# Feed-forward stages of a two-block decoder kernel: the norm's factor per token multiplied in after the up projection

## Chip, cores and metric

The kernel runs on one core of one Trainium2 chip. The metric is the device time of one execution in microseconds (us). The kernel before takes 2204.48 us, the median of 3 runs from 2202.61 to 2205.71.

## What is computed

One sequence of 256 tokens with model width 1024 goes through a first block (feed-forward, state-space mixer, two feed-forwards, attention, feed-forward) and a second block (two mixers and a layer of experts). The change is in the four feed-forward stages, each of which computes

```python
def rmsnorm(x, g):
    xf = x.astype(jnp.float32)
    y = xf * lax.rsqrt(jnp.mean(xf * xf, axis=-1, keepdims=True) + EPS)
    return (y * g.astype(jnp.float32)).astype(x.dtype)

def swiglu_half_step(h, g, w1, w3, w2):
    u = rmsnorm(h, g)
    return h + FFN_HALF * ((jax.nn.silu(u @ w1) * (u @ w3)) @ w2)
```

with h of 256 x 1024, w1 and w3 of 1024 x 2816 and w2 of 2816 x 1024. The stages in order are ffn0, ssm, ffn1, ffn2, kv, attn, ffn3, rwkv, mla, mix, peer. The keys and values come from the h that goes into ffn2, normalised with a gain of their own: TensorE transposes ffn2's normalised rows a second time at ffn2's end (`kv_turn`).

## The kernel before

**Split products.** Every fp32 matrix is held as a rounded part (hi) and a rest (lo), and a product is three matmuls: hi·hi, hi·lo, lo·hi. A weight tile (128 x 1024) comes by DMA into one of four ring slots. ScalarE writes `w_hi[slot]` (`make_hi`, L298), VectorE subtracts to get `w_lo[slot]` (`make_lo`, L303), TensorE multiplies. Each slot has one w_hi and one w_lo: the next tile of the slot is split only when the last product that reads it is done (`split_read`). For a stage's second tile (slot 1) the subtraction at its start is done by GpSimd (`POOL_LEADS`), and for its first tile (slot 0) both halves are made at the end of the stage before. In ffn3 ScalarE makes the hi of slot 1 only after the norm's roots (`LEAD_AFTER_ROOTS`), since the attention stage frees that slot late.

**A feed-forward stage** has 22 tiles of 128 hidden columns. TensorE's order is up(t), down(t-1), up(t+1), down(t), ...: up is 48 matmuls of 256 columns (w1 in slot 0, then w3 in slot 1) into one PSUM bank, down is 12 matmuls of 512 columns (w2 in slot 2 or 3) into four accumulator banks. Between them ScalarE takes silu of the w1 half (L687) and VectorE multiplies it by the w3 half (L709, L710) and splits the result (L712); that is `gate`. At the stage's end the order is up(21), three quarters of down(20), three quarters of down(21), then both last quarters. VectorE adds each finished quarter to h (`update_h`, L592).

**The entry of a stage** (`norm_scalar`, `norm_vector`, `norm_tensor`, `project_first`). h is handled in four quarters: q0 and q1 are the two halves of the width for the first 128 tokens, q2 and q3 for the other 128. ScalarE squares and sums each quarter (L469), and takes Ln and Exp for the factor of each token (L475, L478). VectorE multiplies the rows by it (`rows`, L509, into norm_u), TensorE transposes them (L573), VectorE turns q0 and q2 into `u_hi` with the gain (L514), ScalarE q1 and q3 (L490), VectorE makes `u_lo` of all four in the order q0, q2, q1, q3 (L521, four instructions each). TensorE runs 8 matmuls on zeros ahead of the transposes and 4 between their halves (`keep_busy`, L555). `project_first` then takes tile 0: for w1 and then for w3 eight pairs (L333, L335) with u_hi, the fifth of which waits for ScalarE's quarters; then 16 matmuls with u_lo (L340), the fifth of which waits for all of u_lo. When the first 8 of these are done, slot 0 can be split again for tile 1, and with that the loop begins (L351).

The order on each engine is the order of the code; engines meet only in semaphores.

Of the kernel before, what the change touches and what calls it, by code (L numbers as in the profile page):

```python
# [199 lines left out]
def program(nc, io, stages=STAGES):  # L200
# [31 lines left out]
    with ctx:  # L232
# [230 lines left out]
        def norm_scalar(act, s):  # L463
            m, split = norm_no[s], s in SPLIT_STAGES
            for q in range(4):
                tt = q // 2
# [17 lines left out]
            act.wait_ge(S("in_loaded"), 32)  # L484
            to = u_t if s in PLAIN_STAGES else u_hi
            turned_at = TURNED_OF.get(s, TURNED)
            for q in (1, 3):
                act.wait_ge(S("norm_turned"), 4 * m + q + 1)
                for c in range(4):
                    ins = act.activation(quarter(to, q)[:, c, :], turned_at[q][:, c * P:(c + 1) * P], ACT.Identity,  # L490
                                         scale=V(GAIN[s], 4 + c, 5 + c))
                ins.then_inc(S("u_turned"), 1)
                if s == stages[0]:
                    lead_scalar(act, s, slice(0, 1) if q == 1 else slice(1, None))
# [2531 lines left out]
```

## Time and profile before

| | |
|---|---|
| runs, median of 3 | 2204.48 us (2202.61 to 2205.71) |
| profiled execution, its own time | 2207.05 us |
| its span | 2205.3 us |
| TensorE busy | 2160.1 us, 98% |
| VectorE busy | 1466.5 us, 67% |
| ScalarE busy | 1020.1 us, 46% |
| GpSimd busy | 59.2 us, 3% |
| mean granted TensorE clock | 0.996 of full speed |
| the chain that ended last | 92% TensorE, 4% VectorE, 1% ScalarE |

All times of a trace are microseconds from the span's start. ffn0 enters its loop at 23.6, ffn1 at 411.9, ffn2 at 605.9, ffn3 at 901.6. The page names instructions by the line of the kernel, the engine and what they write and read. "Idle before" in square brackets is how long the engine stood before an instruction, and who released it. The chain of waits lists only what held up the end. The granted clock is given as a share: 1.00 is 2.4 GHz and 0.50 is 1.2 GHz.

### The profile page before, as it was taken

How to read it: one execution, taken by the hardware profiler on the slowest of the kernel's cores; microseconds unless marked ns; L12 is line 12 of the kernel's file. 1: busy time of each engine (PE TensorE's matmuls, PEld its weight loads, DVE VectorE, ACT ScalarE, POOL GpSimd, SP SyncE). 2: the span in 40 equal slices, each digit the busy share in tenths (PEclk: the TensorE clock that was granted, in tenths of full speed). 3: DMA queues.
4: the chain of work that ended last, by engine and by line, in shares of the span. 5: the costliest groups of instructions: out<-in, count | busy, mean ns of one | idle time of the engine just before them, and what ended most of it. 6: DMA issues, size and time to landing. Idle time of an engine off the chain costs nothing.

```text
span 2205.3 us, 42309 instructions
## 1 busy us (share of the span) xinstructions
PE 2160.1 (98%) x15414; PEld 1941.0 (88%) x15428; DVE 1466.5 (67%) x2785; ACT 1020.1 (46%) x1734; POOL 59.2 (3%) x59
## 2 busy tenths in 40 slices
PE   8999999999999999999999899999999999999999
PEld 7999998899899987899998568889889999999998
DVE  5556997655655556655685577989886666666665
ACT  4435766443534346434552353348634444444443
POOL 0000000000010000000000000100000000000000
PEclk9999999999999999999999999999999999999999
DMA  6555664455476534555531024443567666665564
GB/s 210 182 189 176 210 189 143 159 177 192 148 239 199 193 116 141 163 188 182 189 97 52 20 77 146 141 145 138 206 229 234 218 204 207 202 189 189 183 189 134
DMA packets 107726, 374.14 MB, mean 170 GB/s; under 512 B 11984, under 2 KB 17888, under 8 KB 107376
## 3 DMA queue, kind: packets, MB, share of 16 engines
q1 hardware_dynamic: 102848, 354.88, 49.2%
q0 software_dynamic: 4784, 18.00, 2.8%
q8 instruction: 59, 0.97, 0.2%
q14 instruction: 35, 0.29, 0.0%
HBM read 362.29 MB, written 13.69 MB: 170 GB/s over the span
## 4 chain that ended last, share of the span: by engine, by line
PE 92%; DVE 4%; ACT 1%; DVEq 1%; issue 1%; DMA 1%; POOL 0%; ACTq 0%; SPq 0%
PE bank L351 71%; PE bank L380 8%; PE bank L1574 3%; PE bank L2583 3%; DVE w_lo L303 1%; PE bank L555 1%; PE bank L573 1%; ACT w_hi L298 0%; PE bank L2151 0%; PE bank L333 0%; DVE u_lo L521 0%; PE bank L335 0%; PE bank L2535 0%; PE bank L2158 0%; DVE arena L1965 0%
## 5 line engine op out<-in xcount | busy, mean ns | idle before, releaser
L303 DVE TENSOR_TENSOR w_lo<-ring,w_hi 128x1024 fp32r<-128x1024 f32 x576 | 696.4, 1223 | 406.6 <-ACT w_hi L298 404.2
L298 ACT ACTIVATE w_hi<-ring 128x1024 fp32r<-128x1024 f32 x581 | 605.6, 1056 | 617.8 <-PE bank L351 563.9
L351 PE MATMUL bank<-u_hi,w_hi 128*128 128x256 f32 x2568 | 729.0, 284 | 1.9 <-DVE w_lo L303 1.9
L351 PE MATMUL bank<-u_hi,w_lo 128*128 128x256 f32 x2568 | 726.6, 283 | 0.0
L351 PE MATMUL bank<-u_lo,w_hi 128*128 128x256 f32 x2568 | 726.6, 283 | 0.0
L351 PEld LDWEIGHTS bank<-u_hi,w_hi 128*128 128x128 f32 x2568 | 492.1, 192 | 13.0 <-DVE w_lo L303 4.0
L351 PEld LDWEIGHTS bank<-u_lo,w_hi 128*128 128x128 f32 x2568 | 492.2, 192 | 7.4 <-issue 0.5
L351 PEld LDWEIGHTS bank<-u_hi,w_lo 128*128 128x128 f32 x2568 | 492.1, 192 | 0.0
L351 PE MATMUL bank<-w_hi,x_hi 128*128 128x512 f32 x992 | 391.0, 394 | 2.1 <-DVE x_lo L2789 1.3
L351 PE MATMUL bank<-w_lo,x_hi 128*128 128x512 f32 x992 | 388.3, 391 | 0.0
L351 PE MATMUL bank<-w_hi,x_lo 128*128 128x512 f32 x992 | 386.1, 389 | 0.0
L351 PEld LDWEIGHTS bank<-w_hi,x_hi 128*128 128x128 f32 x992 | 187.1, 189 | 39.6 <-issue 2.4
L351 PEld LDWEIGHTS bank<-w_hi,x_lo 128*128 128x128 f32 x992 | 186.4, 188 | 40.4
L351 PEld LDWEIGHTS bank<-w_lo,x_hi 128*128 128x128 f32 x992 | 187.2, 189 | 31.5
L380 PE MATMUL bank<-u_t,ring 128*128 128x256 f32 x928 | 206.1, 380 | 2.2 <-issue 1.8
L380 PEld LDWEIGHTS bank<-u_t,ring 128*128 128x128 f32 x928 | 174.0, 190 | 26.6 <-issue 3.2
L2786 DVE TENSOR_TENSOR x_hi<-arena 128x256 fp32r<-128x256 f32 (+1 forms) x128 | 54.5, 426 | 124.3 <-ACT arena L2649 113.9
L2649 ACT ACTIVATE arena<-bank 128x256 f32<-128x256 f32 x96 | 36.9, 385 | 179.6 <-PE bank L351 179.6
L1574 PE MATMUL bank<-arena 64*64 64x64 f32 (+1 forms) x1888 | 68.2, 229 | 7.6 <-DVE arena L1965 2.1
L1574 PEld LDWEIGHTS bank<-arena 64*64 64x64 f32 x1888 | 63.8, 137 | 13.2 <-ACT arena L1803 2.8
L2583 PEld LDWEIGHTS bank<-arena 128*128 128x128 f32 x512 | 60.2, 192 | 5.4 <-issue 4.0
L2583 PE MATMUL bank<-arena 128*128 128x128 f32 x512 | 62.1, 278 | 2.8 <-issue 1.5
(312 smaller groups left out, 1774.2 us busy)
## 6 DMA issues: line engine op xcount, KB each, us to landing
ring<-in_w SPq DMA_DIRECT2D x264, 512.0 KB, 3.6
ring<-in_expert_u SPq DMA_DIRECT2D x128, 512.0 KB, 3.5
ring<-in_expert_v SPq DMA_DIRECT2D x128, 512.0 KB, 4.2
ring<-in_ssm_in SPq DMA_DIRECT2D x40, 512.0 KB, 4.5
gate_dram<-con SPq DMA_DIRECT2D x16, 576.0 KB, 2.9
arena<-gate_dram POOLq DMA_DIRECT2D x9, 1024.0 KB, 8.5
ring<-in_ssm_out SPq DMA_DIRECT2D x16, 512.0 KB, 4.1
ring<-in_w_o SPq DMA_DIRECT2D x16, 512.0 KB, 3.7
```

The costliest lines, as they stand in the source:

```text
L298: act.activation(w_hi[slot][:, :], ring[slot][:, :], ACT.Copy).then_inc(hi_made[slot], 1)
L303: dve.tensor_tensor(w_lo[slot][:, :], ring[slot][:, :], w_hi[slot][:, :].bitcast(F32), ALU.subtract).then_inc(freed[slot], 1)
L351: mm = pe.matmul(out, left[a], right[b], start=start and n == 0, stop=stop and n == 2, skip_group_check=True)
L380: mm = pe.matmul(out, ring[slot][:, c * width:(c + 1) * width], u_t[:, c, :], start=(c == 0), stop=(c == DC - 1))
L555: pe.matmul(bank[4][:, :], zeros[:, 0:P], zeros[:, :], start=True, stop=True)
L573: mm = pe.transpose(TURNED_OF.get(s, TURNED)[q][:, c * P:(c + 1) * P], norm_u[:, q // 2, at:at + P], C("ident"))
L1574: mm = pe.matmul(bank[b][a, at:at + width], left[a, :], right[a, :], start=(n == 0), stop=(n == len(products) - 1))
L2583: mm = pe.matmul(ROT[g][:, t * P:(t + 1) * P], one_b[:, g, t, :], one_a[:, g, t, :], start=True, stop=True)
L2649: act.activation(gelu_buf[:, n, :], ROT[n][:, 0:T], ACT.Gelu).then_inc(S("gelu_out"), 1)
L2786: dve.tensor_tensor(chunks(x_hi[:, n:n + 1, :]), chunks(src), gates, ALU.mult)
```

## The change

For the four feed-forward stages (`LATE_SCALE`):

- TensorE transposes h itself, as soon as a quarter of h is updated; `rows` and the zero matmuls of the entry are gone (12 ahead of ffn0's transposes stay, and 4 behind them). ffn2 still makes its rows, for kv, but behind its u_lo.
- The products are made with h times the gain, without the factor per token. ScalarE writes the factors as a diagonal matrix of 128 x 128 for each half of the tokens (`diag`), TensorE multiplies it by ones between the fourth and fifth pair of the w3 tile (`spread_roots`), so that every partition of bank 0 holds the 256 factors, and VectorE copies that to `root_t`, ahead of the last quarter of u_lo.
- ScalarE squares the last quarter and takes the second root only after its two quarters of u_hi.
- In `gate`, VectorE first multiplies the whole up tile (512 columns: w1 and w3 halves) by root_t into SBUF (`scaled_up`), then ScalarE takes silu from there, then VectorE goes on as before. In the kernel before, silu read PSUM as soon as the tile was done.

```diff
+LATE_SCALE = ("ffn0", "ffn1", "ffn2", "ffn3")
...
         def project_first(pe, stage, *products, one_bank=False, between=None):
...
+                    if between and (n, c) == (1, 4):
+                        between()
...
         def norm_scalar(act, s):
             for q in range(4):
                 tt = q // 2
+                if late and q == 3:
+                    turned(1)
+                    turned(3)
...
-                    act.activation(stat[:, 10 + tt:11 + tt], stat[:, 8 + tt:9 + tt], ACT.Exp,
-                                   scale=-0.5).then_inc(S("norm_root"), 1)
+                    ins = act.activation(stat[:, 10 + tt:11 + tt], stat[:, 8 + tt:9 + tt], ACT.Exp, scale=-0.5)
+                    if late:
+                        act.drain()
+                        act.wait_ge(S("in_loaded"), 32)
+                        ins = act.activation(diag[:, tt, :], C("ident"), ACT.Copy, scale=stat[:, 10 + tt:11 + tt])
+                    ins.then_inc(S("norm_root"), 1)
             if s in LEAD_AFTER_ROOTS:
                 lead_scalar(act, s, slice(LEAD_BEFORE[s], 2))
...
+            if not late:
+                turned(1)
+                turned(3)
...
         def norm_vector(dve, s):
-            rows(0)
+            if s not in LATE_SCALE:
+                rows(0)
...
                 for q in (0, 2, 1, 3):
+                    if q == 3 and s in LATE_SCALE:
+                        dve.wait_ge(S("norm_turned"), turned_before(s) + 5)
+                        dve.tensor_copy(root_t, bank[0][:, 0:T])
                     lo(q)
+                if s == HOLDS_KV:
+                    rows(0)
+                    rows(1)
...
         def norm_tensor(pe, s):
-            elif not calm:
+            elif not calm and s not in LATE_SCALE:
                 keep_busy(pe, 8)
             for q in range(4):
-                if q == 2 and not calm:
+                if q == 2 and not calm and s not in LATE_SCALE:
                     keep_busy(pe, 4)
...
-                pe.wait_ge(S("norm_rows"), 4 * norm_no[s] + (4 if s == "attn" else q + 1))
+                if s in LATE_SCALE:
+                    pe.wait_ge(S(("h_loaded", "h_moved")[q // 2]), 16)
+                    pe.wait_ge(S("h_updated"), max(4 * upd[s] - 2 + q, 1))
+                else:
+                    pe.wait_ge(S("norm_rows"), rows_before(s) + (4 if s == "attn" else q + 1))
...
         def ffn_tensor(pe, k, updates):
+            def spread_roots():
+                for tt in range(TT):
+                    pe.wait_ge(S("norm_root"), 2 * norm_no[stage] + tt + 1)
+                    mm = pe.matmul(bank[0][:, tt * P:(tt + 1) * P], C("ones"), diag[:, tt, :], start=True, stop=True)
+                mm.then_inc(S("norm_turned"), 1)
...
         def ffn_scalar(act, k):
             def silu(b, i):
-                split_done(act, *ffn_tile(1, k, i, b))
-                act.activation(silu_buf[:, b, :], UP[b][:, 0:T], ACT.Silu).then_inc(S("silu_ready"), 1)
+                act.wait_ge(S("up_scaled"), FC * ffn_no[stage_of(k)] + 2 * i + b + 1)
+                act.activation(silu_buf[:, b, :], scaled_up[:, b, 0:T], ACT.Silu).then_inc(S("silu_ready"), 1)
...
         def ffn_vector(dve, k):
             def gate(b, i):
+                split_done(dve, *ffn_tile(1, k, i, b))
+                dve.tensor_tensor(scaled_up[:, b, :].rearrange("p (n t) -> p n t", n=2),
+                                  UP[b][:, :].rearrange("p (n t) -> p n t", n=2),
+                                  root_t.unsqueeze(1).broadcast_to([P, 2, T]), ALU.mult).then_inc(S("up_scaled"), 1)
                 dve.wait_ge(S("silu_ready"), base + 2 * i + b + 1)
...
-                dve.tensor_tensor(x_hi[:, b, :], silu_buf[:, b, :], UP[b][:, T:2 * T], ALU.mult)
-                dve.tensor_tensor(hid_buf[:, b, :], silu_buf[:, b, :], UP[b][:, T:2 * T], ALU.mult)
+                dve.tensor_tensor(x_hi[:, b, :], silu_buf[:, b, :], scaled_up[:, b, T:2 * T], ALU.mult)
+                dve.tensor_tensor(hid_buf[:, b, :], silu_buf[:, b, :], scaled_up[:, b, T:2 * T], ALU.mult)
```

The rest of the diff renames two semaphores of the state-space stage into one and counts the semaphores anew.

**ScalarE at ffn3's entry.** L469/L500 are the squares, L478/L509 the Exp, L490/L487 the quarters of u_hi, L298/L299 the hi of a weight tile (first slot 1, then slot 2). Before:

```order
L469 ACTIVATE arena,stat<-h 128x512 [waits h_updated,h_moved]
L475 ACTIVATE stat<-stat 128x1
L478 ACTIVATE stat<-stat 128x1
L298 ACTIVATE w_hi<-ring 128x1024 [waits split_read1,slot_full1]
L490 ACTIVATE u_hi<-bank,vec 128x128 [waits norm_turned,in_loaded]
L490 ACTIVATE u_hi<-bank,vec 128x128 x3
L490 ACTIVATE u_hi<-bank,vec 128x128 [waits norm_turned]
L490 ACTIVATE u_hi<-bank,vec 128x128 x3
L298 ACTIVATE w_hi<-ring 128x1024 [waits split_read2,slot_full2]
```

And now, L513 being a diagonal:

```order
L487 ACTIVATE u_hi<-bank,vec 128x128 [waits norm_turned]
L487 ACTIVATE u_hi<-bank,vec 128x128 x3
L487 ACTIVATE u_hi<-bank,vec 128x128 [waits norm_turned]
L487 ACTIVATE u_hi<-bank,vec 128x128 x3
L500 ACTIVATE arena,stat<-h 128x512 [waits h_updated,h_moved]
L506 ACTIVATE stat<-stat 128x1
L509 ACTIVATE stat<-stat 128x1
L513 ACTIVATE arena<-con,stat 128x128 [waits in_loaded]
L299 ACTIVATE w_hi<-ring 128x1024 [waits split_read1,slot_full1]
L299 ACTIVATE w_hi<-ring 128x1024 [waits split_read2,slot_full2]
```

The hi of slot 1 stood ahead of the quarters of u_hi; it now stands behind them, behind the last square, the second root and its diagonal.

**VectorE at ffn2's entry**, from its quarters of u_hi (L514/L541) on; L521/L548 is u_lo, L581 the copy of the spread factors, L509/L536 the rows. Before:

```order
L514 TENSOR_TENSOR u_hi<-bank,vec 128x4x128 [waits norm_turned]
L521 SCALAR_TENSOR_TENSOR u_lo<-bank,vec,u_hi 128x128 x8
L521 SCALAR_TENSOR_TENSOR u_lo<-bank,vec,u_hi 128x128 [waits u_turned]
L521 SCALAR_TENSOR_TENSOR u_lo<-bank,vec,u_hi 128x128 x3
L521 SCALAR_TENSOR_TENSOR u_lo<-bank,vec,u_hi 128x128 [waits u_turned]
L521 SCALAR_TENSOR_TENSOR u_lo<-bank,vec,u_hi 128x128 x3
L303 TENSOR_TENSOR w_lo<-ring,w_hi 128x1024 [waits hi_made2]
```

And now:

```order
L541 TENSOR_TENSOR u_hi<-bank,vec 128x4x128 [waits norm_turned] x2
L548 SCALAR_TENSOR_TENSOR u_lo<-bank,vec,u_hi 128x128 x8
L548 SCALAR_TENSOR_TENSOR u_lo<-bank,vec,u_hi 128x128 [waits u_turned]
L548 SCALAR_TENSOR_TENSOR u_lo<-bank,vec,u_hi 128x128 x3
L581 COPY arena<-bank 128x256 [waits norm_turned]
L548 SCALAR_TENSOR_TENSOR u_lo<-bank,vec,u_hi 128x128 [waits u_turned]
L548 SCALAR_TENSOR_TENSOR u_lo<-bank,vec,u_hi 128x128 x3
L536 TENSOR_SCALAR arena<-h,stat 128x512 [waits norm_root]
L536 TENSOR_SCALAR arena<-h,stat 128x512
L536 TENSOR_SCALAR arena<-h,stat 128x512 [waits norm_root]
L536 TENSOR_SCALAR arena<-h,stat 128x512
L304 TENSOR_TENSOR w_lo<-ring,w_hi 128x1024 [waits hi_made2]
```

The copy stands between the third and fourth quarter of u_lo and waits for TensorE. The four rows moved from ahead of u_hi to behind u_lo, and only in ffn2; the other three feed-forward stages have none.

**VectorE at the last tile of ffn0**, up to the update of h. Before:

```order
L709 TENSOR_TENSOR x_hi<-arena,bank 128x256 [waits split_read3,silu_ready]
L710 TENSOR_TENSOR arena<-arena,bank 128x256
L712 TENSOR_TENSOR x_lo<-arena,x_hi 128x256
L592 SCALAR_TENSOR_TENSOR h<-bank,h 128x512 [waits acc_done] x3
```

And now:

```order
L757 TENSOR_TENSOR arena<-bank,arena 128x512 [waits split_read1]
L762 TENSOR_TENSOR x_hi<-arena 128x256 [waits split_read3,silu_ready]
L763 TENSOR_TENSOR arena<-arena 128x256
L765 TENSOR_TENSOR x_lo<-arena,x_hi 128x256
L632 SCALAR_TENSOR_TENSOR h<-bank,h 128x512 [waits acc_done] x3
```

The multiplication by the factors (L757) is new; ScalarE's silu stands between it and x_hi.

## Rows read from the trace of the kernel before

**Rows 1.** The page: busy time of each engine.

```profile
PE 2160.1 (98%) x15414; PEld 1941.0 (88%) x15428; DVE 1466.5 (67%) x2785; ACT 1020.1 (46%) x1734; POOL 59.2 (3%) x59
```

**Rows 2.** Timeline, end of ffn1: start, duration, engine, line, out<-in.

```profile
588.00 0.38 ACT L687 ACTIVATE arena<-bank 128x256 f32<-128x256 f32 x1 [1.76 <-PE bank L351]
...
589.25 0.43 DVE L712 TENSOR_TENSOR x_lo<-arena,x_hi 128x256 fp32r<-128x256 f32 x1
...
589.64 0.40 PE L351 MATMUL bank<-w_hi,x_lo 128*128 128x512 f32 x1
...
589.88 0.40 PE L351 MATMUL bank<-w_hi,x_hi 128*128 128x512 f32 x1
```

**Rows 3.** Groups by shape: count | busy us, mean ns | idle before.

```profile
L514 DVE TENSOR_TENSOR u_hi<-bank,vec 128x512 fp32r<-128x512 f32 x12 | 8.3, 692 | 8.2 <-PE bank L573 8.2
...
L429 ACT ACTIVATE x_hi<-arena 128x256 fp32r<-128x256 f32 x8 | 3.2, 414 | 6.2 <-PE bank L351 6.2
```

**Rows 4.** Timeline, ffn2's end: VectorE turning the kv quarters.

```profile
785.35 1.29 DVE L733 TENSOR_TENSOR u_t<-bank,vec 128x512 f32<-128x512 f32 x2 [0.55 <-PE bank L619]
```

**Rows 5.** Timeline, middle of ffn1's loop, VectorE and ScalarE.

```profile
489.43 0.42 DVE L709 TENSOR_TENSOR x_hi<-arena,bank 128x256 fp32r<-128x256 f32 x1
...
491.68 1.06 ACT L298 ACTIVATE w_hi<-ring 128x1024 fp32r<-128x1024 f32 x1 [3.34 <-PE bank L351]
```

**Rows 6.** Chain of waits at ffn1's entry: start, us, what.

```profile
399.62 1.67 PE bank L555 x7
401.30 0.87 PE bank L573 x8
...
404.44 0.36 PE bank L333
...
408.51 0.97 PE bank L340 x8
...
409.57 1.07 ACT w_hi L298
...
410.66 1.24 DVE w_lo L303
```

**Rows 7.** Timeline, ffn1's entry, VectorE and ScalarE.

```profile
400.20 0.87 DVE L509 TENSOR_SCALAR arena<-h,stat 128x512 f32<-128x512 f32 x2
...
400.87 0.61 ACT L469 ACTIVATE arena<-h 128x512 f32<-128x512 f32 x1
...
402.01 0.20 ACT L478 ACTIVATE stat<-stat 128x1 f32<-128x1 f32 x1
...
404.40 4.23 DVE L521 SCALAR_TENSOR_TENSOR u_lo<-bank,vec,u_hi 128x128 fp32r<-128x128 f32 x16
```

**Rows 8.** Chain of waits at ffn3's entry.

```profile
889.24 1.67 PE bank L555 x7
...
901.56 23.49 PE bank L351 x170
```

**Rows 9.** Timeline, ffn3's entry, ScalarE and GpSimd.

```profile
891.74 1.04 ACT L298 ACTIVATE w_hi<-ring 128x1024 fp32r<-128x1024 f32 x1
892.69 2.15 ACT L490 ACTIVATE u_hi<-bank,vec 128x128 fp32r<-128x128 f32 x8
...
892.87 2.38 POOL L303 TENSOR_TENSOR w_lo<-ring,w_hi 128x1024 fp32r<-128x1024 f32 x1 [212.38 <-ACT w_hi L298]
```

**Rows 10.** Timeline, ffn0's entry, TensorE.

```profile
8.33 1.94 PE L573 MATMUL bank<-con,arena 128*128 128x128 f32 x8 [2.45 <-DMA vec<-in_vecs]
```

**Rows 11.** Stretches: busy (x) of PE, PEld, DVE, ACT, POOL; PEclk, DMA share, GB/s.

```profile
9.00:10.00 1.00, 1.00 (x6) 1.00 (x6) 0.47 (x1) 0.25 (x2) 0.00 (x0) 0.50 1.03 422
...
12.00:13.00 1.00, 1.00 (x10) 0.86 (x9) 0.56 (x1) 0.58 (x2) 0.00 (x0) 1.00 0.89 127
...
859.00:860.00 1.00, 0.62 (x3) 0.63 (x4) 1.00 (x4) 0.17 (x1) 0.00 (x0) 0.50 0.47 123
...
864.00:865.00 1.00, 1.00 (x4) 0.67 (x2) 0.00 (x0) 1.00 (x5) 0.00 (x0) 0.50 0.10 25
```

More of the change, by code:

```diff
@@ L323, in lead_next_hi, with project_first @@
                 lead_scalar(act, stage, slice(0, LEAD_BEFORE.get(stage, 0)))
-        def project_first(pe, stage, *products, one_bank=False):
+        def project_first(pe, stage, *products, one_bank=False, between=None):
             for n, (out, slot, ring_stage, i, nth) in enumerate(products):
@@ L453, in program, with rows_before, turned_before @@
         HOLDS_KV = "ffn2"
+        diag, root_t = area(20000, 2, P), area(20256, T)
+        scaled_up = area(20512, 2, 2 * T)
+        rows_made = [s for s in norm_no if s not in LATE_SCALE or s == HOLDS_KV]
+        def rows_before(s):
+            return 4 * len([x for x in rows_made if norm_no[x] < norm_no[s]])
+        def turned_before(s):
+            return 4 * norm_no[s] + len([x for x in LATE_SCALE if norm_no[x] < norm_no[s]])
         def quarter(u, q):
@@ L464, in norm_scalar, with turned @@
             m, split = norm_no[s], s in SPLIT_STAGES
+            late = s in LATE_SCALE
+            to = u_t if s in PLAIN_STAGES else u_hi
+            turned_at = TURNED_OF.get(s, TURNED)
+            def turned(q):
+                act.wait_ge(S("norm_turned"), turned_before(s) + q + 1)
+                for c in range(4):
+                    ins = act.activation(quarter(to, q)[:, c, :], turned_at[q][:, c * P:(c + 1) * P], ACT.Identity,
+                                         scale=V(GAIN[s], 4 + c, 5 + c))
+                ins.then_inc(S("u_turned"), 1)
+                if s == stages[0]:
+                    lead_scalar(act, s, slice(0, 1) if q == 1 else slice(1, None))
             for q in range(4):
                 tt = q // 2
+                if late and q == 3:
+                    turned(1)
+                    turned(3)
                 act.wait_ge(S(("h_loaded", "h_moved")[tt]), 16)
@@ L483, in norm_scalar @@
                 kv_squares(act)
[L484 to L494, printed above, removed]
+            if not late:
+                turned(1)
+                turned(3)
             if split and s in PLAIN_STAGES:
@@ L543, in norm_vector @@
                 turned(0, u_hi)
-                rows(1)
+                if s not in LATE_SCALE:
+                    rows(1)
                 turned(2, u_hi)
@@ L614, in kv_turn @@
         def kv_turn(pe, q):
+            if q == 0:
+                pe.wait_ge(S("norm_rows"), rows_before(HOLDS_KV) + 4)
             if q >= 2:
@@ L656, in down @@
                 close_split(pe, b, 2 + b, stage, i, last, quarters)
+            def spread_roots():
[3 more added lines that the diff above has]
+                mm.then_inc(S("norm_turned"), 1)
             pe.wait_ge(S("hid_ready"), base + 1)
-            project_first(pe, stage, *((UP[0][:, n * T:(n + 1) * T], *ffn_tile(n, k, 0, 0)) for n in range(2)), one_bank=True)
+            project_first(pe, stage, *((UP[0][:, n * T:(n + 1) * T], *ffn_tile(n, k, 0, 0)) for n in range(2)), one_bank=True,
+                          between=spread_roots)
             clear_acc(pe, updates)
```

14 lines of the change are left out of this document (8 added, 6 removed).

## Prediction, made blind

> **What bounds the kernel now.** I read the page first: TensorE is busy for 2160.1 of 2205.3 us, VectorE for two thirds, ScalarE for half [rows 1]. Inside the loops of a feed-forward stage the chain of waits is unbroken TensorE work. So only the seams can give time, and only what TensorE waits for there counts. Then I read the timeline and the chain around the four entries and four ends of the feed-forward stages, and last the granted clock where TensorE had stood idle.
>
> An end: TensorE issues the last of nine matmuls of down(20) at 589.64 and the first of down(21) at 589.88, on its normal pitch, while VectorE's x_lo ends at 589.68 [rows 2]. The cover is 0.2 us. An entry, counted from t = 0 when TensorE starts its zero matmuls (399.62): transposes at 1.7, first products at 4.8, products with u_lo from 8.9, the first half of these done at 9.9; then hi and lo of slot 0 (1.07 and 1.24), and the loop begins at 12.3 [rows 6]. ffn3 is the same, 889.24 to 901.56 [rows 8].
>
> **The change part by part.** I work in one clock, that of the profiled execution.
>
> *In the loop.* VectorE gets one more instruction per tile. A product of 512 elements from PSUM takes it 0.69 us [rows 3]. Each tile lasts 8.5 us (48 products at 0.12 and 12 at 0.23), of which VectorE works some 5 (three subtractions of 1.23 and 1.25 for gate). In the loop its gate starts at 489.43 when both weight subtractions are done, not when silu is. Now: scale 489.4 to 490.1, silu from SBUF (0.41, the like row of rows 3) to 490.6, three steps of gate (1.25 as from silu's end to x_lo's end less a hop) to 491.9. VectorE's next work waits for the hi that ScalarE starts at 491.68 and ends at 492.7 [rows 5], so 0.8 us are spare, and the down product needs gate's result only at about 494.5, after up(t+1). The loop costs nothing. Uncovered, all of it would be 88 x 0.69 = 61 us.
>
> *The ends.* There the same insertion has 0.2 us of cover. From the end of the last up product the chain was silu, x_hi, hid, x_lo (588.00 to 589.68 [rows 2]); it becomes scale, silu, x_hi, hid, x_lo. Added: 0.69, one hop between engines of 0.04 (silu's end 588.38 to the next engine's start is of this size), and 0.06 because silu and x_hi read SBUF. That is 0.8, less 0.2 of cover: 0.6 us each for ffn0, ffn1 and ffn3. ffn2 has the kv transposes in between; there VectorE's work on the kv quarters comes 0.8 later, and TensorE's third kv transpose waits for the first of them. These take 1.29 for two [rows 4]; I take 0.4. Ends together: 3 x 0.6 + 0.4 = +2.2. Below zero is excluded, as nothing at the ends is removed; at most it is 4 x 0.8 = 3.2.
>
> *ffn1's entry.* TensorE transposes q0 to q2 from t = 0, four in 0.44 (8 in 0.87 [rows 6]), so 1.3; q3 behind the update of h, to 1.75. VectorE's second u_hi is done at 2.3 and the first product starts at 2.4, against 4.8. ScalarE: diagonal 0.35 (estimated from a 128 x 128 piece of 0.28, four in 1.14), third square to 1.6, u_hi's two quarters to 3.75, then last square to Exp's end 1.34 (400.87 to 402.21 [rows 7]) and a second diagonal: 5.45. The fifth pair therefore waits for ScalarE until 3.8; the w3 tile's fourth pair is done at 5.9 and the factors are there. VectorE: three quarters of u_lo at 1.05 each (4.23 for four [rows 7]) from 2.3 to 5.5, then it stands until the spread product (5.9 to 6.2) has landed, copies (0.35, estimated from the 0.42 of x_hi with its overlap), and makes the last quarter from 6.75 to 7.8. TensorE's fifth u_lo product goes at 7.85, the half is done at 8.5 against 9.9. From there on hi and lo follow as before. Gain 1.4, not the 2.4 of the earlier start: the copy and its wait stand in front of the last quarter.
>
> *ffn2's entry.* The same, but four rows (0.87 for two [rows 7], so 1.75) now stand behind u_lo: 7.8 to 9.6, slot 2's subtraction to 10.8, and slot 0's to 12.0, where ScalarE's hi would have allowed 9.7. The loop begins at 12.1 instead of 12.5. Gain 0.4.
>
> *ffn3's entry.* Here the order on ScalarE decides. The hi of slot 1 ran at 891.74, t = 2.5, and GpSimd's subtraction from 892.87 for 2.38 us to t = 6.0 [rows 9]; the w3 tile started at about 7.0 (4.8, 16 pairs' halves at 0.12, and 0.25 for the first), so it had 1.0 us of cover. Now that hi stands behind u_hi's quarters, the last square, the root and its diagonal: 5.45 to 6.5, and GpSimd 6.6 to 9.0. TensorE's w1 pairs are done at 4.95, and it stands idle for 4.0 us. Then four pairs to 10.0, spread 10.25, copy 10.75, last quarter of u_lo 11.85, half done 12.55 against 9.9. That is +2.7.
>
> *The clock in ffn3.* In ffn0 TensorE stood 2.45 us ahead of its first transposes [rows 10] and found 1.2 GHz; it was back at 2.4 by 12 [rows 11]. In attention, after a stretch with many holes, it ran at 1.2 from 859 to 865 [rows 11]. A hole of 4.0 us should do the same. The pairs then take 0.24 instead of 0.12. If it recovers 3.3 us after work resumes, as in ffn0, half of w3's pairs and part of the rest are slow, +1.4; if after 6.4, as in attention, +2.8. Between 0 (it holds) and 2.8 I take 2.1.
>
> *ffn0's entry* is bound by its weights: slot 1's lo comes at 15.8 instead of 16.2, but the factor's copy takes 0.4 back. 0, within -0.3 to +0.5.
>
> *The zero matmuls.* Without them the entries of ffn1 and ffn2 have holes of 0.6 and 0.3 us between bursts of work. I cost them at nothing, since the transposes keep TensorE going for the first 1.75 us; what it costs if not is the second rival.
>
> **Sum.** Ends +2.2, ffn0 0, ffn1 -1.4, ffn2 -0.4, ffn3 +2.7 and +2.1: +5.2 us. The profiled execution would go from 2207.05 to 2212.2. It was itself 2.6 above the median of the runs, so the median goes from 2204.48 to 2209.7.
>
> **Rivals.**
>
> *A. The clock holds in ffn3's hole.* For it: the two low stretches followed the kernel's start and a stretch of many small holes, not a hole in the middle of dense work. Against it: the one clean hole there is, 2.45 us, was followed by 1.2 GHz, and this one is longer. +3.1, so 2207.6.
>
> *B. The clock falls at ffn1's and ffn2's entries as well.* This needs transposes not to keep it up: then TensorE does next to nothing that counts from t = 0 to 2.4, as long as in ffn0's hole. For it: in ffn0 eight transposes and four zero matmuls ran at the low clock before it rose, so the rows can't tell which of them raised it. Against it: the hole is filled, and products follow at 2.4. Each entry would lose what I took for ffn3, 2.1: +9.4, so 2213.9. The Trainium skill (page "TensorE: Matmul & The Clock Gate", Part 4, PE-mode transpose) states that the full clock "doesn't engage" for transposes, as they don't count as busy in the same way. By that rule this rival is the likely one. No row here shows transposes alone for long enough, so the trace neither agrees nor disagrees.
>
> *C. The other side: the entries are bound by their start.* If TensorE, not VectorE's copy, set the pace, ffn1, ffn2 and ffn3 would each be 2.4 us shorter. The point that decides is whether the w3 tile's lo is there at t = 5 in ffn3 and the last quarter of u_lo before TensorE gets to it, in ffn1 and ffn2. For it: the first product does start 2.4 earlier. Against it: VectorE's 4.2 us of u_lo already ended only just ahead of its readers, and GpSimd's 2.38 us can't start before ScalarE. 2.2 - 7.2 = -5.0, so 2199.5.
>
> *D. The loop does not hide the scale.* Every row of the loop leaves 0.8 us, but if the extra hop to ScalarE delayed the next hi by half a us per tile, 88 tiles would add 44 to the forecast: 2253.7.
>
> **How the numbers follow.** My forecast 0.52, A 0.13, B 0.22, C 0.09, D 0.04. A change within 0.2%, 4.4 us, can't be told from none in this kernel. The forecast's own spread is 2.5 either way (ends 0 to 3.2, clock 0 to 2.8, estimated copies and diagonals), from 2207.2 to 2212.2; about 0.3 of its 0.52 lies above 2208.9. Slower: 0.32 + B 0.22 + D 0.04 = 0.58. Same: 0.20 + A 0.13 + 0.02 of C = 0.35. Faster: 0.07. The range takes in A and B and leaves out most of C and D: 2204.0 to 2215.5.
>
> **What would show it.** In ffn3, TensorE idle about 4 us ahead of the first pair of the w3 tile, released by GpSimd's w_lo, and the loop beginning 15 to 17.5 us after t = 0; the clock at half behind it. In ffn1 the loop beginning near 10.9, with VectorE standing before its copy; in ffn2 near 12.1, with the rows between u_lo and slot 2. At the ends of ffn0, ffn1 and ffn3, TensorE waiting some 0.6 us for x_lo ahead of down(21). In the loops, spacing of 8.5 us per tile as before. I am wrong if slot 1's lo is there earlier in ffn3, if the low clock shows in ffn1 or ffn2, or if the loops got longer.

## The result, and the profile after

| | before | changed |
|---|---|---|
| median (lowest to highest), 12 runs each | 2203.64 us (2200.12 to 2205.71) | 2208.20 us (2206.02 to 2210.82) |
| ratio, 95% interval | | 1.0021 [1.0013, 1.0029] |
| profiled execution (span) | 2207.05 us (2205.3) | 2207.07 us (2205.3) |

The changed kernel is slower by 4.6 us, 0.21%. The forecast was +5.2 us and a median of 2209.7 (2204.0 to 2215.5).

The page of the changed kernel: VectorE has 58 us more work [rows 1], the 88 new scales above all, and TensorE 5 us less, since 36 zero matmuls are gone.

```profile
PE 2155.0 (98%) x15404; PEld 1938.5 (88%) x15404; DVE 1524.7 (69%) x2865; ACT 1035.3 (47%) x1742; POOL 59.3 (3%) x59
```

**An end.** The timeline of the changed kernel at ffn1's end, which answers to [rows 2]. L757 is the scale, L736 silu, L762 and L765 x_hi and x_lo, L354 the product.

```profile
585.80 0.69 DVE L757 TENSOR_TENSOR arena<-bank,arena 128x512 f32<-128x512 f32 x1 [0.37 <-PE bank L354]
...
586.53 0.42 ACT L736 ACTIVATE arena<-arena 128x256 f32<-128x256 f32 x1 [2.48 <-DVE arena L757]
...
586.98 0.43 DVE L762 TENSOR_TENSOR x_hi<-arena 128x256 fp32r<-128x256 f32 x1 [0.48 <-ACT arena L736]
...
587.44 0.39 PE L354 MATMUL bank<-w_hi,x_lo 128*128 128x512 f32 x1
587.81 0.43 DVE L765 TENSOR_TENSOR x_lo<-arena,x_hi 128x256 fp32r<-128x256 f32 x1
...
588.29 0.50 PE L354 MATMUL bank<-w_hi,x_hi 128*128 128x512 f32 x1 [0.46 <-DVE x_lo L765]
```

TensorE now stands 0.46 us before the last down product, where it stood not at all. The cost is a little more than the number in brackets: from the product before it, at 587.44, to this one are 0.85 us, where they were 0.24 in the kernel before. From the loop's start to the stage's last product ffn1 takes 182.11 us instead of 181.35, ffn3 182.07 instead of 181.35: +0.7 each, as in ffn0. ffn2, with its kv transposes in between, takes 0.6 more.

**ffn1's entry.** The chain of waits of the changed kernel, which answers to [rows 6]. The transposes start at 398.21, so t is the time less 398.21.

```profile
400.76 1.56 ACT u_hi L487 x6
...
402.37 0.39 PE bank L336
...
404.54 0.46 PE bank L703 x4
...
405.02 0.42 DVE arena L581
405.44 1.04 DVE u_lo L548 x4
...
406.53 0.76 PE bank L343 x4
...
409.74 0.51 PE bank L354 x2
```

Here one reads the price of the copy directly: the spread product (L703), the copy (L581) and the last quarter of u_lo (L548) stand one behind the other in front of the fifth product with u_lo. The loop begins at t = 11.53 instead of 12.3. (The table below counts from the end of the stage before. In the kernel before, its zero matmuls start 0.23 us behind that, so there 12.3 is 12.54; in the changed kernel the transposes start at once.)

**ffn2's entry.** VectorE in the timeline of the changed kernel; the rows for kv are L536.

```profile
594.16 3.19 DVE L548 SCALAR_TENSOR_TENSOR u_lo<-bank,vec,u_hi 128x128 fp32r<-128x128 f32 x12
598.63 0.42 DVE L581 COPY arena<-bank 128x256 f32<-128x256 f32 x1 [1.28 <-PE bank L703]
598.97 1.12 DVE L548 SCALAR_TENSOR_TENSOR u_lo<-bank,vec,u_hi 128x128 fp32r<-128x128 f32 x4
600.00 1.67 DVE L536 TENSOR_SCALAR arena<-h,stat 128x512 f32<-128x512 f32 x4
601.59 3.49 DVE L304 TENSOR_TENSOR w_lo<-ring,w_hi 128x1024 fp32r<-128x1024 f32 x3
```

The wait of 1.28 us, the rows and the subtractions (601.59 on) follow each other without a gap; the loop begins at t = 12.14.

**ffn3's entry.** ScalarE, GpSimd and TensorE in the timeline of the changed kernel, the transposes from 886.90 on, which answers to [rows 8, 9].

```profile
888.85 2.15 ACT L487 ACTIVATE u_hi<-bank,vec 128x128 fp32r<-128x128 f32 x8
...
892.32 0.40 ACT L513 ACTIVATE arena<-con,stat 128x128 f32<-128x128 f32 x1
892.62 1.99 ACT L299 ACTIVATE w_hi<-ring 128x1024 fp32r<-128x1024 f32 x2
893.75 2.34 POOL L304 TENSOR_TENSOR w_lo<-ring,w_hi 128x1024 fp32r<-128x1024 f32 x1 [215.14 <-ACT w_hi L299]
...
896.15 0.38 PE L336 MATMUL bank<-u_hi,w_hi 128*128 128x256 f32 x1 [3.87 <-POOL w_lo L304]
...
897.09 0.41 PE L338 MATMUL bank<-u_hi,w_lo 128*128 128x256 f32 x1
```

The stretches of the same place (columns as in [rows 11]) show the clock behind the hole:

```profile
896.00:897.00 1.00, 0.85 (x5) 0.86 (x6) 0.00 (x0) 0.00 (x0) 0.09 (x1) 0.76 0.00 0
897.00:898.00 1.00, 1.00 (x7) 1.00 (x6) 0.00 (x0) 0.00 (x0) 0.00 (x0) 0.50 0.96 143
...
899.00:900.00 1.00, 1.00 (x6) 1.00 (x6) 1.00 (x5) 0.00 (x0) 0.00 (x0) 0.54 0.05 21
900.00:901.00 1.00, 1.00 (x11) 1.00 (x10) 1.00 (x3) 0.00 (x0) 0.00 (x0) 1.00 0.00 0
```

TensorE stands 3.87 us until GpSimd's subtraction lands, and is at 1.2 GHz from its first products behind it until 899.9. The loop begins at 903.72, t = 16.82, instead of 12.3.

**The stages as a table.** Entry: from the end of the stage before (for ffn0 from its first transpose) to the loop's first product. Loop and end: from there to the stage's last product. All numbers are differences of start times in the timelines, in us; "whole" spans from ffn0's first transpose to ffn3's last product; the last column leaves the state-space stage, kv and attention out of it, and is given against before. "Combined" is there twice, from two profiles. The other rows are the experiments of the next section.

| kernel | entry ffn0 | entry ffn1 | entry ffn2 | entry ffn3 | loop and end, ffn1 | whole | the four stages |
|---|---|---|---|---|---|---|---|
| before | 15.28 | 12.54 | 12.59 | 12.55 | 181.35 | 1074.58 | 0 |
| changed | 14.50 | 11.53 | 12.14 | 16.82 | 182.11 | 1078.54 | +4.8 |
| only ffn3 | 15.26 | 12.55 | 12.59 | 17.22 | 181.33 | 1080.22 | +5.4 |
| without ffn3 | 14.50 | 11.53 | 12.17 | 12.54 | 182.09 | 1074.08 | -0.2 |
| lead first | 14.52 | 11.53 | 12.17 | 12.48 | 182.10 | 1074.94 | +0.6 |
| hole filled | 14.31 | 11.54 | 12.15 | 15.67 | 182.10 | 1078.30 | +3.5 |
| scale in halves | 14.30 | 11.53 | 12.17 | 17.31 | 181.82 | 1077.74 | +4.0 |
| copy behind | 14.13 | 11.16 | 11.16 | 16.70 | 182.12 | 1076.31 | +3.0 |
| scale three times | 14.30 | 11.54 | 12.16 | 16.93 | 184.00 | 1087.30 | +14.1 |
| combined | 13.97 | 11.16 | 11.18 | 12.10 | 181.82 | 1070.83 | -2.9 |
| combined, again | 13.96 | 11.15 | 11.16 | 12.10 | 181.87 | 1071.63 | -2.9 |

Over the whole stretch the changed kernel takes 4.0 us more. Its four stages take 4.8 more, near the difference of the medians, 4.6; attention took 0.8 less, mostly because in its profile the clock was low there for 3.4 us and in that of before for 6.8. In attention this differs from profile to profile whatever the kernel, so the last column is the one to compare. That the two profiled executions are equal to 0.02 us is chance. The first transposes start at 8.33 in before and 7.25 in the changed kernel, when a transfer has landed, and behind ffn3 before loses another 2.9 us. The clock fell there at 1224, in one of the mixers, where the same work ran at 2.4 GHz in the changed kernel. Before:

```profile
1224.00:1226.00 2.00, 1.22 (x24) 1.03 (x23) 0.69 (x1) 1.97 (x4) 0.00 (x0) 0.50 0.04 8
```

Changed:

```profile
1226.00:1228.00 2.00, 1.21 (x33) 1.00 (x30) 0.71 (x2) 1.97 (x4) 0.00 (x0) 1.00 0.00 0
```

And at the entry of rwkv a weight came late for ScalarE in before and in time in the changed kernel. The timelines, before and then changed:

```profile
1098.26 1.06 ACT L298 ACTIVATE w_hi<-ring 128x1024 fp32r<-128x1024 f32 x1 [1.01 <-DMA ring<-in_rwkv_in]
```

```profile
1100.17 1.05 ACT L299 ACTIVATE w_hi<-ring 128x1024 fp32r<-128x1024 f32 x1
```

These are 15.35 and 14.38 us behind ffn3's last product. In 6 of the 10 profiles other than that of "scale three times" this wait is there, in 4 not, with no relation to the edits that I can see.

### The profile page after: what moved, and what is told of

It reads as the page before. It is cut to its first block, busy times and chain, and to the rows that moved or that the text cites. A ratio compares the mean times of both kernels' runs of the same rounds, so it can differ in the third digit from the quotient of the medians.

```text
span 2205.3 us, 42449 instructions
## 1 busy us (share of the span) xinstructions
PE 2155.0 (98%) x15404; PEld 1938.5 (88%) x15404; DVE 1524.7 (69%) x2865; ACT 1035.3 (47%) x1742; POOL 59.3 (3%) x59
## 4 chain that ended last, share of the span: by engine, by line
PE 91%; DVE 5%; ACT 2%; issue 1%; DVEq 1%; ACTq 0%; DMA 0%; POOL 0%; SPq 0%
PE bank L354 70%; PE bank L383 8%; PE bank L2636 3%; PE bank L1627 3%; DVE w_lo L304 1%; PE bank L336 0%; PE bank L338 0%; ACT w_hi L299 0%; PE bank L590 0%; PE bank L2204 0%; PE bank L613 0%; PE bank L2588 0%; PE bank L2211 0%; DVE arena L2018 0%; PE bank L343 0%
## 5 line engine op out<-in xcount | busy, mean ns | idle before, releaser
L299 ACT ACTIVATE w_hi<-ring 128x1024 fp32r<-128x1024 f32 x581 | 605.4, 1056 | 431.9 <-PE bank L354 392.2
L354 PE MATMUL bank<-u_hi,w_hi 128*128 128x256 f32 x2568 | 729.0, 284 | 2.4 <-DVE w_lo L304 2.4
L354 PE MATMUL bank<-u_hi,w_lo 128*128 128x256 f32 x2568 | 726.6, 283 | 0.0
L354 PE MATMUL bank<-u_lo,w_hi 128*128 128x256 f32 x2568 | 726.6, 283 | 0.0
L354 PEld LDWEIGHTS bank<-u_hi,w_hi 128*128 128x128 f32 x2568 | 492.1, 192 | 13.7 <-DVE w_lo L304 4.6
L354 PEld LDWEIGHTS bank<-u_lo,w_hi 128*128 128x128 f32 x2568 | 492.1, 192 | 7.4 <-issue 0.5
L354 PEld LDWEIGHTS bank<-u_hi,w_lo 128*128 128x128 f32 x2568 | 492.1, 192 | 0.0
L354 PE MATMUL bank<-w_hi,x_hi 128*128 128x512 f32 x992 | 390.9, 394 | 3.5 <-DVE x_lo L765 1.4
L354 PE MATMUL bank<-w_lo,x_hi 128*128 128x512 f32 x992 | 388.2, 391 | 0.0
L354 PE MATMUL bank<-w_hi,x_lo 128*128 128x512 f32 x992 | 386.1, 389 | 0.0
L354 PEld LDWEIGHTS bank<-w_hi,x_hi 128*128 128x128 f32 x992 | 187.0, 188 | 41.7 <-DVE x_lo L765 2.7
L354 PEld LDWEIGHTS bank<-w_hi,x_lo 128*128 128x128 f32 x992 | 186.3, 188 | 40.4
L354 PEld LDWEIGHTS bank<-w_lo,x_hi 128*128 128x128 f32 x992 | 187.0, 189 | 31.5
L736 ACT ACTIVATE arena<-arena 128x256 f32<-128x256 f32 x88 | 36.8, 418 | 185.8 <-DVE arena L757 185.8
L762 DVE TENSOR_TENSOR x_hi<-arena 128x256 fp32r<-128x256 f32 x88 | 37.5, 426 | 46.2 <-ACT arena L736 46.2
```

The lines of the kernel that those rows point to most:

```text
L299: act.activation(w_hi[slot][:, :], ring[slot][:, :], ACT.Copy).then_inc(hi_made[slot], 1)
L354: mm = pe.matmul(out, left[a], right[b], start=start and n == 0, stop=stop and n == 2, skip_group_check=True)
L736: act.activation(silu_buf[:, b, :], scaled_up[:, b, 0:T], ACT.Silu).then_inc(S("silu_ready"), 1)
L762: dve.tensor_tensor(x_hi[:, b, :], silu_buf[:, b, :], scaled_up[:, b, T:2 * T], ALU.mult)
```

## The experiments

The theory: the loss is in ffn3's entry, where the hi of slot 1 stands behind the roots on ScalarE (a hole, and a low clock after it), and 0.7 at each end; the entries of ffn1 and ffn2 give some back, and the loop is neutral. Rivals were that the clock falls at the other entries too, that the loop pays for the scale, and that the hole costs only through the clock or only through the order. Ratios are to before, timed on the same chip. They are those on record; the quotient of two medians differs from them by up to 0.001. Medians of different rows come from different chips, where before itself had 2203.63 to 2204.52.

**Only ffn3, and all but ffn3.** `LATE_SCALE` is cut to one stage or to three, with the branches that let the other stages run as before.

```diff
-LATE_SCALE = ("ffn0", "ffn1", "ffn2", "ffn3")
+LATE_SCALE = ("ffn3",)                    # only_ffn3
+LATE_SCALE = ("ffn0", "ffn1", "ffn2")     # without_ffn3
```

> Only ffn3 is changed, ffn0 to ffn2 are as before. Theory 1 (the slowdown is ffn3's entry, where the w3 tile waits for GpSimd behind ScalarE's new order): ffn3's loop begins 16.8 us after the last product of attention, as in the changed kernel, its end costs 0.6 more, and the time is 5 us above the kernel before. Theory 2 (each changed stage costs the same, through the multiplication ahead of silu): a quarter of the change's +4.6, so about +1.2.

> ffn0, ffn1 and ffn2 are changed, ffn3 is as before. Theory 1: entries ffn0 -0.8, ffn1 -0.8, ffn2 -0.3 and ends +0.6, +0.55, +0.6, so -0.2 against the kernel before: no difference that can be measured. Theory 2: three quarters of +4.6, so +3.5.

Measured: only ffn3 2207.34 us, 1.0016 [1.0006, 1.0025]; without ffn3 2206.38 us, 1.001 [1.0, 1.002]. In the table's last column ffn3 alone carries the whole loss, +5.4, and the other three stages together come to -0.2: entries -0.8, -1.0 and -0.4, ends +0.7, +0.7 and +0.6. That is 5.2 together against 4.8 of the changed kernel. The 0.4 between them is the entry of ffn3, 17.22 against 16.82, where the clock was low for longer (below). The medians agree less well: without ffn3 lies about 2 us above what its stages give, which the section on the hardware takes up.

**The hi of slot 1 ahead of ScalarE's quarters of u_hi** in ffn3, with the rest as changed:

```diff
                 if late and q == 3:
+                    if s in LEAD_AFTER_ROOTS:
+                        lead_scalar(act, s, slice(LEAD_BEFORE[s], 2))
                     turned(1)
                     turned(3)
...
-            if s in LEAD_AFTER_ROOTS:
+            if s in LEAD_AFTER_ROOTS and not late:
```

> The changed kernel, but ScalarE makes the hi of slot 1 in ffn3 ahead of its quarters of u_hi, as before. Theory 1: GpSimd's w_lo is done at about t = 5.3, TensorE waits under 0.5 us ahead of the w3 tile, the clock stays at full, and ffn3's loop begins near t = 12 (u_hi's quarters come 1 us later, and the last square behind them too), 4.8 earlier than in the changed kernel: about equal to the kernel before, -4.5 against the changed one. Rival (the hole comes from the factors' chain, since the diagonal is as late as ever): the hole stays or moves to the spread product, and less than 1.5 us come back.

Measured: 2205.17 us, 1.0002 [0.9993, 1.0011], 3.0 us below the changed kernel's median; by the two ratios it is 0.0019, 4.2 us. The timeline of this kernel at ffn3's entry, transposes from 887.74 on (the end of the stage before is at 887.52):

```profile
889.47 1.04 ACT L299 ACTIVATE w_hi<-ring 128x1024 fp32r<-128x1024 f32 x1
...
890.42 2.15 ACT L487 ACTIVATE u_hi<-bank,vec 128x128 fp32r<-128x128 f32 x8
890.60 2.36 POOL L304 TENSOR_TENSOR w_lo<-ring,w_hi 128x1024 fp32r<-128x1024 f32 x1 [208.04 <-ACT w_hi L299]
...
892.62 0.39 PE L336 MATMUL bank<-u_hi,w_hi 128*128 128x256 f32 x1 [1.57 <-ACT u_hi L487]
```

GpSimd is done at 892.96, before TensorE needs it; what is left is 1.57 us ahead of the fifth pair of w1, and the granted clock is 1.00 in every stretch from 890 to 896. The entry takes 12.48 instead of 16.82. One instruction moved past the others on its engine takes away all of the loss of ffn3's entry, hole and clock; its end still costs 0.7.

**The hole filled.** TensorE runs 16 matmuls on zeros ahead of its wait for the w3 tile; nothing on the other engines changes.

```diff
         def project_first(...):
...
+                if n == 1 and stage == "ffn3":
+                    for _ in range(16):
+                        pe.matmul(bank[1][:, :], zeros[:, 0:P], zeros[:, :], start=True, stop=True)
                 multiplied(pe, slot, ring_stage, i, nth)
```

> The changed kernel with 16 matmuls on zeros between ffn3's w1 and w3 tiles, so that TensorE is at work in the hole. If the clock falls for the hole, it now stays at full: the pairs of the w3 tile take 0.12 and not 0.21 each, and the loop begins near t = 15.3 instead of 16.8: -1.5 us. If the clock falls for another reason, the w3 tile still runs at half, and the loop begins at 16.8 as before.

Measured: 2209.32 us, 1.002 [1.0011, 1.0029]; the entry 15.67 instead of 16.82. The timeline and then the stretches of this kernel:

```profile
892.68 3.63 PE L331 MATMUL bank<-zeros 128*128 128x512 bf16 x16
896.72 0.39 PE L339 MATMUL bank<-u_hi,w_hi 128*128 128x256 f32 x1 [0.41 <-POOL w_lo L304]
```

```profile
897.00:898.00 1.00, 1.00 (x11) 1.00 (x11) 0.00 (x0) 0.00 (x0) 0.00 (x0) 1.00 0.63 78
```

With the hole filled the clock holds. So the low clock follows from the hole and costs 1.15 us here; the other 3.1 of the entry are the order itself. The kernels "only ffn3" and "scale in halves" have the same hole, and their entries are dearer than this one by 1.55 and 1.64: their clock was low from inside the hole until 4.3 and 4.6 us behind its end, against 3.8 in the changed kernel. The gain of 1.15 can't be seen in the median, which is even 1.1 above the changed kernel's, within its interval.

**The scale in two halves**, w1's first, so that silu starts sooner:

```diff
-                dve.tensor_tensor(scaled_up[:, b, :]..., UP[b][:, :]..., root_t..., ALU.mult).then_inc(S("up_scaled"), 1)
+                dve.tensor_tensor(scaled_up[:, b, 0:T], UP[b][:, 0:T], root_t, ALU.mult).then_inc(S("up_scaled"), 1)
+                dve.tensor_tensor(scaled_up[:, b, T:2 * T], UP[b][:, T:2 * T], root_t, ALU.mult)
+                dve.drain()
```

> The changed kernel with the multiplication by the factors in two: first the w1 half (256 columns), which releases silu, then the w3 half beside silu. Theory (the ends cost what stands between the last up product and x_lo): from the start of the first multiplication to x_hi 0.9 us instead of 1.18, so each of the ends of ffn0, ffn1 and ffn3 is 0.3 us shorter and the loops are as before: -1 us in all against the changed kernel. Rival (the ends wait for something else, a slot or a weight): no stage gets shorter.

Measured: 2207.37 us, 1.0014 [1.0005, 1.0022]. Its timeline at ffn1's end:

```profile
585.48 0.42 DVE L757 TENSOR_TENSOR arena<-bank,arena 128x256 f32<-128x256 f32 x1 [0.50 <-PE bank L354]
...
585.93 0.42 ACT L736 ACTIVATE arena<-arena 128x256 f32<-128x256 f32 x1 [2.22 <-DVE arena L757]
...
587.70 0.50 PE L354 MATMUL bank<-w_hi,x_hi 128*128 128x512 f32 x1 [0.20 <-DVE x_lo L765]
```

TensorE's wait for x_lo falls from 0.46 to 0.20 and the stage by 0.3. The end is indeed the chain scale, silu, x_hi, x_lo.

**The copy behind the last quarter of u_lo**, where nothing of the entry waits for it:

```diff
                 for q in (0, 2, 1, 3):
-                    if q == 3 and s in LATE_SCALE:
-                        dve.wait_ge(S("norm_turned"), turned_before(s) + 5)
-                        dve.tensor_copy(root_t, bank[0][:, 0:T])
                     lo(q)
+                if s in LATE_SCALE:
+                    dve.wait_ge(S("norm_turned"), turned_before(s) + 5)
+                    dve.tensor_copy(root_t, bank[0][:, 0:T]).then_inc(S("up_scaled"), 1)
```

TensorE waits for it before it clears its accumulators, and the counts of `up_scaled` go up by one per stage. VectorE also drains once more, behind its subtractions for tile 1.

> The changed kernel with VectorE's copy of the spread factors behind the last quarter of u_lo instead of ahead of it (TensorE's clearing of bank 0 waits for it). Theory (the copy and its wait for the spread product stand in front of the u_lo that TensorE waits for): u_lo is complete near t = 6.7 instead of 8.3, TensorE does not wait in its u_lo products, and the loops of ffn1 and ffn3 begin 0.8 to 1.0 earlier (ffn1: 10.7 us after t = 0); ffn2 gains nothing beyond 0.3, since its rows stand behind u_lo all the same. Rival (the entry is bound by TensorE's own products and by ScalarE): under 0.2 each.

Measured: 2207.06 us, 1.001 [1.0002, 1.0019]. ffn1's entry gained 0.37 and ffn3's 0.12, less than the expected 0.8 to 1.0, ffn2's 1.0, more, and ffn0's 0.37. The chain of waits of this kernel at ffn1's entry:

```profile
405.65 0.12 PE bank L338
405.77 0.97 PE bank L343 x8
...
406.82 1.07 ACT w_hi L299
```

The u_lo products now follow the last pair at once: with the copy away TensorE itself sets ffn1's entry, and only 0.37 us lay between the two. In ffn2 it was VectorE that set it, with the rows and subtractions in its queue, so most of the 1.28 us that it had stood before the copy comes back.

**The scale three times.** Two more scales of the same size per tile, into areas that nobody reads:

```diff
+                dve.tensor_tensor(more_a[:, b, :]..., UP[b][:, :]..., root_t..., ALU.mult)
+                dve.tensor_tensor(more_b[:, b, :]..., UP[b][:, :]..., root_t..., ALU.mult)
                 dve.tensor_tensor(scaled_up[:, b, :]..., UP[b][:, :]..., root_t..., ALU.mult).then_inc(S("up_scaled"), 1)
```

> The changed kernel with the multiplication by the factors done three times per tile (twice into unused space), so 1.4 us more of VectorE's time in each of the 88 tiles. Theory (the loop hides it, VectorE has 8.5 us per tile and needs 7.1): the loops keep 8.5 us per tile, and only the ends grow, by 1.4 us each in ffn0, ffn1 and ffn3 and by 0.7 to 1.4 in ffn2: +5 to +6 us against the changed kernel. Rival (VectorE's extra time reaches TensorE in the loop): up to 88 x 1.4 = 120 us more.

Measured: 2215.78 us, 1.0046 [1.0033, 1.006], 7.6 above the changed kernel, or 1.9 per stage (5.5 by the two ratios). In the trace the four stages take 9.3 more. 1.6 of this is a low clock at ffn0's end. The timeline of this kernel at ffn1's end:

```profile
590.19 0.68 DVE L758 TENSOR_TENSOR arena<-bank,arena 128x512 f32<-128x512 f32 x1
...
592.10 0.42 ACT L737 ACTIVATE arena<-arena 128x256 f32<-128x256 f32 x1 [3.50 <-DVE arena L764]
...
593.86 0.50 PE L354 MATMUL bank<-w_hi,x_hi 128*128 128x512 f32 x1 [2.39 <-DVE x_lo L772]
```

The wait at the end went from 0.46 to 2.39, and ffn1's loop and end together by the same 1.9. So 22 tiles with 1.2 us more of VectorE each cost TensorE nothing inside the loop: it has room for three scales, not only one. Of the 1.9 at the end 1.2 are the two scales at their pitch of 0.60; the rest is that the first one no longer waits for TensorE but for VectorE's own subtractions.

**Combined.** The hi first, the scale in halves, the copy behind, ffn2's rows behind its subtraction for tile 1, and 12 zero matmuls instead of 4 behind ffn0's transposes. It was timed twice.

> Four mends of the changed kernel together: slot 1's hi ahead of u_hi's quarters in ffn3, the multiplication in halves, the copy behind u_lo, and ffn2's rows moved into the loop's start (behind the weights of tile 1); and eight more matmuls on zeros in the hole of ffn0's entry, where the clock fell. Theory: against the changed kernel ffn3's entry -5, ends -1.2, ffn1's entry -0.9, ffn2's -0.8, ffn0's -1.5: some -9 us, so 2199, 4 to 5 us below the kernel before. If the parts don't add up because the same u_lo or weights bind again: 2202, about 2 below the kernel before.

> The same kernel as the one called combined, timed a second time, since its first profile showed 3.75 us less than before from the first transposes to the entry of the stage behind ffn3 (1070.83 against 1074.58 us), and yet its median stood at 0.9998 of before. Theory 1: the gain is in the feed-forward stages and is hidden by where the granted clock falls later, which differs from run to run: that span is again within 0.3 us of 1070.8, the time at 0.50 behind it differs from the first profile's, and the ratio lies between 0.9985 and 1.0000. Theory 2: the kernel shifts the later stages so that the clock falls there more often: the same later stretches (1218 to 1226, 1242 to 1248, 1460 to 1466 us) are low again, and the ratio is again 0.9995 to 1.0005.

Measured: 2204.50 us, 0.9998 [0.9989, 1.0007], and 2204.34 us, 0.9999 [0.999, 1.0008]: no different from before. All four entries are shorter than before, and the four stages by 2.9 us in both profiles. The stretch to ffn3's last product is shorter by 3.75 and 2.95; the 0.8 between the two profiles is attention, where the clock was low for 3.4 us in the first and 6.8 in the second. Next to nothing of the gain reaches the median. In both profiles the clock fell again later, among others here (first and second profile), where the changed kernel had 1.00:

```profile
1244.00:1246.00 2.00, 2.00 (x3) 0.57 (x2) 1.03 (x2) 0.41 (x1) 0.00 (x0) 0.50 0.00 0
```

```profile
1240.00:1242.00 2.00, 2.00 (x3) 0.88 (x4) 0.87 (x2) 1.01 (x2) 0.00 (x0) 0.51 0.00 0
```

Low stretches of both profiles also begin at 1461 and 1458, and this place is low in no other kernel's profile. That they recur speaks for the second theory of the last expectation. That the first profile's at 1218 did not speaks for the first. So does that its two low stretches at 1219 and 1243 are not the combined kernel's own: counted from ffn3's last product they begin about 140 and 164 us behind it, and so do two in the kernel with the hole filled. The ratio lay where both would have it. The section on the hardware has what the other runs add.

## Why the prediction was right

The sign, the size and the place held. The terms add up to +5.2 as forecast and +4.8 as measured in the four stages, but the nearness is in part luck: the ends and the order in ffn3 cost 0.6 and 0.4 more than forecast, and ffn1's entry gave 0.4 less, while ffn0's entry gave 0.8 that was not forecast and the clock cost 0.9 less.

- **The loop: 0.** Right. VectorE had 0.8 us to spare by the forecast; the tripled scale shows that there are at least 1.2 more. Rival D is refuted.
- **The ends: +0.6 each, +2.2 together.** Measured +0.73 in ffn0, +0.76 in ffn1 and +0.72 in ffn3, by the chain named, and +0.57 in ffn2, where +0.4 was taken: +2.8 together. Halving the scale took back 0.3, as the chain says.
- **ffn0's entry: 0.** Wrong, -0.8, and in all versions with a late scale in ffn0 (only ffn3 keeps 15.26). What failed is the size of what the earlier weights gave: 0.4 was taken, and the copy was to take it back. The timelines, before and then changed, show VectorE's subtraction for slot 1, behind which u_lo begins:

```profile
14.99 1.23 DVE L303 TENSOR_TENSOR w_lo<-ring,w_hi 128x1024 fp32r<-128x1024 f32 x1 [0.54 <-ACT w_hi L298]
```

```profile
12.60 1.23 DVE L304 TENSOR_TENSOR w_lo<-ring,w_hi 128x1024 fp32r<-128x1024 f32 x1 [0.75 <-ACT w_hi L299]
```

  It ends 7.89 and 6.58 us behind the first transpose (8.33 and 7.25), so it came 1.3 earlier. From there to the loop it is 0.5 longer for the copy, near the 0.4 of the forecast, and 0.8 is left.
- **ffn1's entry: -1.4.** Measured -1.0. The mechanism is right. Three times that were estimated were short, by 0.64 together, and the loop began at 11.53 instead of 10.9: ScalarE's quarters released the fifth pair at t = 4.16, not 3.8; the spread products took 0.46, not 0.25; the copy 0.42, not 0.35.
- **ffn2's entry: -0.4.** Measured -0.45, with VectorE's queue as the bound as said.
- **ffn3's entry: +2.7 and clock +2.1, 4.8 together.** Measured +4.27, made up otherwise: 3.1 order and 1.15 clock. The idle time was 3.87 (forecast 4.0), released by GpSimd. The clock was back 3.8 us behind the hole's end (3.1 to 4.6 in the five profiles with the hole), so the recovery of ffn0 was the better of the two models; the 1.4 that it gave was the nearer value, and I took 2.1 between it and attention's. The order was dearer by 0.4, about 0.3 of it the longer spread product, copy and diagonal.
- **Rival A** (the clock holds in the hole) is refuted: it fell in all five profiles that have the hole, and in none of the six without it.
- **Rival B** (the clock falls at ffn1 and ffn2 too) is refuted. The Trainium skill's page "TensorE: Matmul & The Clock Gate" (Part 4, PE-mode transpose), by which the full clock doesn't engage for transposes, had made it likely. These are the stretches of the changed kernel from its transposes on:

```profile
398.00:400.00 2.00, 2.00 (x18) 1.78 (x16) 1.57 (x3) 1.73 (x8) 0.00 (x0) 1.00 0.71 170
400.00:402.00 2.00, 1.30 (x10) 1.01 (x8) 1.90 (x7) 2.00 (x9) 0.00 (x0) 1.00 0.49 201
402.00:404.00 2.00, 1.63 (x13) 1.64 (x14) 1.71 (x7) 1.79 (x8) 0.00 (x0) 1.00 0.04 8
```

  The trace doesn't bear the rule out here, but it doesn't test it alone either: no run has transposes without products near them. What the runs show is that an entry whose first 1.9 us are transposes and whose holes are 0.44 and 0.62 us keeps 2.4 GHz, in ffn1 and ffn2 of all nine profiles that have the late scale there.
- **Rival C** (the entries bound by their start) is refuted for the kernel as changed, and its deciding point was well placed: with w3's lo early and the copy away, the combined kernel has entries of 11.16, 11.18 and 12.10, shorter than before by 1.4, 1.4 and 0.45. That is still not the 2.4 each.

## What to carry to other kernels

A new factor behind a product costs nothing in a loop where the engine that applies it has slack in every tile, and nearly its full chain at the loop's end, where little stands beside it: count the ends apart from the loop. Where a step moves later on an in-order engine, look at what is queued behind it for another engine; here one weight split behind a root made 4.3 of the 4.8 us, and moving it ahead again gave 4.3 back in the trace and 3.0 in the median. Before a change at this scale is judged by its median, compare the stages that it touches between the traces, and leave out what lies between them.

## What the runs showed of the hardware

- **The granted clock falls at different places in different executions of one kernel, and this is most of the spread of its times.** The two profiles of the combined kernel show it (1219, 1243 and 1461 against 1240 and 1458 us). From ffn3's last product to the end, the four profiles without a low stretch before the very end take 1119.1 to 1119.6 us, the seven with one 1121.7 to 1126.7; six of the seven also have the late weight of rwkv. Of 29 runs of before timed beside the combined kernel, those with a mean clock of 0.996 took 2206.1 us on average (5), 0.998 2202.9 (9) and 1.0 2200.3 (2): 6 us between the ends, more than the change itself.
- **The later stages hide part of what an earlier one saves.** The combined kernel's 2.9 us and the 0.2 of the version without ffn3 don't appear in their medians, which lie 3.8, 3.2 and 2.0 us above the median of before less this gain; by the ratios it is about 2.5 each, with intervals of 2 us either way. A part of it is the clock: the combined kernel's runs have a mean of 0.9966 and 0.9965, before on the same chips 0.9974 and 0.9971. By the numbers above 0.001 goes with 1.6 us, so this is some 1.1 to 1.3 us. Why these runs had the lower clock, and where the rest went, no run here shows.
- **A hole of 3.87 us lost the clock in five profiles of five, one of 1.57 us (the hi first, and both combined) in none of three; between them it went either way.** At ffn0's entry a hole of 1.86 us was followed by 1.2 GHz in four profiles of seven. With the scale three times, the ends of ffn0, ffn1 and ffn3 have a hole of 2.39 us each behind dense work, and only the one of ffn0 was followed by it:

```profile
202.30 0.50 PE L354 MATMUL bank<-w_hi,x_hi 128*128 128x512 f32 x1 [2.39 <-DVE x_lo L772]
```

```profile
204.00:206.00 2.00, 2.00 (x6) 1.51 (x6) 0.99 (x2) 1.74 (x5) 1.78 (x1) 0.50 0.00 0
```

- **A product of 128 x 128 fp32 by ones for two halves of the tokens is four records and 0.46 us**, where I had estimated 0.25 (0.85 at 1.2 GHz, in the kernel with the copy behind), and a ScalarE scaling of 128 x 128 within SBUF 0.40.
